# Rounded products that stream their columns from last to first

## What is computed

```python
for l in range(2):
    x = x + 0.5 * g1 * swiglu(modulate(x, sh1, sc1), ffn1_gate[l], ffn1_up[l], ffn1_down[l])
    x = x + g2 * token_mix(modulate(x, sh2, sc2), ...)       # w_in, gates, w_branch, w_out
    x = x + 0.5 * g3 * swiglu(modulate(x, sh3, sc3), ffn2_gate[l], ffn2_up[l], ffn2_down[l])
x = rms_norm(x) * final_norm
x = x + merged(rms_norm_2(x) @ w_in_2, ...) @ w_o_2          # four branches, gated and summed
x = x + square(relu(rms_norm_2(x) @ w_up_2)) @ w_down_2
```

## Time and profile before

| | |
|---|---|
| median of 3 runs | 3470.61 us (3468.1 to 3471.58) |
| span of the profiled execution | 3462.0 us, first to last instruction (the page gives no time of its own for it; the median lies 8.6 us above the span) |
| TensorE (PE) busy | 3417.4 us, 99% of the span |
| weight loads (PEld) busy | 2737.1 us, 79% |
| VectorE (DVE) / ScalarE (ACT) / GpSimd (POOL) busy | 51% / 35% / 8% |
| mean granted TensorE clock | 0.995 of full speed |
| DMA | 376.36 MB, a third of the 16 engines' span |

### The profile page before, as it was taken

How to read it: one execution, slowest core, us unless ns; L and a number is a source line. 1 busy time by engine, 2 the same in 40 slices (tenths; PEclk the granted TensorE clock), 3 DMA queues, 4 the chain that set the end, 5 groups by cost and what they waited for, 6 DMA issues and landing times.

```text
span 3462.0 us, 40836 instructions
## 1 busy us (share of the span) xinstructions
PE 3417.4 (99%) x16686; PEld 2737.1 (79%) x16686; DVE 1754.0 (51%) x3014; ACT 1197.3 (35%) x2021; POOL 263.1 (8%) x219
## 2 busy tenths in 40 slices
PE   8999999999999999999999999999999999999999
PEld 7888786778888788887767888888778777878887
DVE  7666446555565733334655643334453555364433
ACT  3222336543222332223555332224322444233322
POOL 0000210002000200011100100003011000120000
PEclk9999999999999999999999999999999999999999
DMA  7555322123565532323211322322222223122332
GB/s 253 203 208 192 108 84 69 41 71 112 190 228 194 183 100 95 104 86 117 74 44 31 105 90 83 106 87 96 77 79 68 76 67 122 39 96 90 98 103 79
DMA packets 120361, 376.36 MB, mean 109 GB/s; under 512 B 13296, under 2 KB 28272, under 8 KB 120176
## 3 DMA queue, kind: packets, MB, share of 16 engines
q1 hardware_dynamic: 120176, 373.76, 32.8%
HBM read 371.61 MB, written 2.10 MB: 108 GB/s over the span
## 4 chain that ended last, share of the span: by engine, by line
PE 93%; DVE 4%; ACT 2%; issue 0%; DMA 0%; POOL 0%; SPq 0%; DVEq 0%; ACTq 0%; POOLq 0%
PE ps L449 27%; PE ps L451 26%; PE ps L450 26%; PE ps L671 2%; PE ps L694 2%; PE ps L566 2%; PE ps L483 1%; PE ps L485 1%; PE ps L484 1%; PE ps L499 1%; DVE s_wl L1490 1%; PE ps L492 1%; ACT s_wh L969 0%; PE ps L536 0%; PE ps L537 0%
## 5 line engine op out<-in xcount | busy, mean ns | idle before, releaser
L1490 DVE TENSOR_TENSOR s_wl<-s_raw,s_wh 128x1024 fp32r<-128x1024 f32 (+3 forms) x645 | 705.7, 1095 | 885.2 <-ACT s_wh L969 878.7
L449 PE MATMUL ps<-s_uh,s_wh 128*128 128x512 f32 x2824 | 1128.5, 400 | 9.7 <-DVE s_ul L1551 3.8
L451 PE MATMUL ps<-s_ul,s_wh 128*128 128x512 f32 x2824 | 1104.2, 391 | 0.8 <-issue 0.8
L450 PE MATMUL ps<-s_uh,s_wl 128*128 128x512 f32 x2824 | 1103.4, 391 | 0.0
L969 ACT ACTIVATE s_wh<-s_raw 128x1024 fp32r<-128x1024 f32 (+3 forms) x645 | 588.1, 913 | 723.0 <-PE ps L451 535.4
L449 PEld LDWEIGHTS ps<-s_uh,s_wh 128*128 128x128 f32 x2824 | 532.2, 188 | 152.8 <-issue 40.2
L451 PEld LDWEIGHTS ps<-s_ul,s_wh 128*128 128x128 f32 x2824 | 531.7, 188 | 113.6 <-issue 1.2
L450 PEld LDWEIGHTS ps<-s_uh,s_wl 128*128 128x128 f32 x2824 | 532.5, 189 | 107.3 <-issue 2.7
L449 PE MATMUL ps<-s_fh,s_wh 128*128 128x512 f32 x960 | 378.6, 394 | 0.0
L451 PE MATMUL ps<-s_fl,s_wh 128*128 128x512 f32 x960 | 378.6, 394 | 0.0
L450 PE MATMUL ps<-s_fh,s_wl 128*128 128x512 f32 x960 | 378.6, 394 | 0.0
(11 more groups left out here) (419 smaller groups left out, 3337.9 us busy)
## 6 DMA issues: line engine op xcount, KB each, us to landing
s_raw<-w SPq DMA_DIRECT2D x616, 512.0 KB, 3.6
s_raw<-w SPq DMA_DIRECT2D x96, 192.0 KB, 2.4
s_raw<-w SPq DMA_DIRECT2D x64, 256.0 KB, 2.6
s_raw<-w SPq DMA_DIRECT2D x19, 128.0 KB, 2.0
s_x<-x SPq DMA_DIRECT2D x4, 512.0 KB, 6.7
out<-s_x SPq DMA_DIRECT2D x8, 256.0 KB, 2.2
s_raw<-w SPq DMA_DIRECT2D x4, 420.0 KB, 4.2
s_crow<-crow SPq DMA_DIRECT2D x2, 512.0 KB, 6.0
```

Of the source, the lines that this page charges most:

```text
L449: TE.matmul(o, w_hi(i, k), h, start=first, stop=False)
L450: TE.matmul(o, w_lo(i, k), h, start=False, stop=False)
L451: return TE.matmul(o, w_hi(i, k), l, start=False, stop=last)
L1490: V.tensor_tensor(wl[w][:, 0:n], raw[t % NRAW][:, 0:n], wh[w][:, 0:n].bitcast(F32), SUB).then_inc(*s_lo.up(("lo", t)))
```

## The change

A helper turns a view round in its last dimension, and every rounded product takes its moving operand and its output through it. The stationary operand stays as it was. So column 511 is streamed first and its results go to column 511 of the bank, then 510, and so on to 0 (279 to 0 for the short ones). Each column still meets the same weights and lands at the same place. The float32 products are left alone, and so are all readers of the banks.

```diff
+def back(t):
+    return t[:, ::-1]
...
         def three(o, i, k, h, l, first, last):
+            o, h, l = back(o), back(h), back(l)
             TE.matmul(o, w_hi(i, k), h, start=first, stop=False)
             TE.matmul(o, w_lo(i, k), h, start=False, stop=False)
             return TE.matmul(o, w_hi(i, k), l, start=False, stop=last)
...
-                        TE.matmul(o, h[:, k, sl(b)], w_hi(i, j), start=k == 0, stop=False)
-                        TE.matmul(o, l[:, k, sl(b)], w_hi(i, j), start=False, stop=False)
-                        ins = TE.matmul(o, h[:, k, sl(b)], w_lo(i, j), start=False, stop=k == nk - 1)
+                        TE.matmul(back(o), h[:, k, sl(b)], back(w_hi(i, j)), start=k == 0, stop=False)
+                        TE.matmul(back(o), l[:, k, sl(b)], back(w_hi(i, j)), start=False, stop=False)
+                        ins = TE.matmul(back(o), h[:, k, sl(b)], back(w_lo(i, j)), start=False, stop=k == nk - 1)
...
-                        TE.matmul(os[n][:], h, uh[:, k, :], start=k == 0, stop=False)
-                        TE.matmul(os[n][:], lo, uh[:, k, :], start=False, stop=False)
-                        ins = TE.matmul(os[n][:], h, ul[:, k, :], start=False, stop=k == 7)
+                        TE.matmul(back(os[n]), h, back(uh[:, k, :]), start=k == 0, stop=False)
+                        TE.matmul(back(os[n]), lo, back(uh[:, k, :]), start=False, stop=False)
+                        ins = TE.matmul(back(os[n]), h, back(ul[:, k, :]), start=False, stop=k == 7)
```

## The result

The changed kernel takes **3520.98 us** (median of 4, 3516.09 to 3523.46) against 3471.1 us before (median of 4, 3468.1 to 3481.73). The ratio is 1.0125, with a 95% interval of 1.0102 to 1.0149: slower by a little over one per cent. The profiled execution has a span of 3519.1 us, 57.1 us more than before. The forecast was no difference.

The account below looks back on a forecast made before the run. TensorE was taken to bound the kernel, through the start-to-start distance of 13,032 rounded products. Span 3462.0 + 0 for the change, plus 8.6 us from span to median, gave 3470.6 us; range 3,385 to 3,545 us.

Parts of the forecast that it names:

- The bound: Whole kernel: TensorE sets the time, PE busy 99% of the span, with 13,032 rounded products counted by start-to-start distance.
- Between these I take **zero: Rounded products: a descending stream adds nothing to the start-to-start distance, chosen between a 3,266 us floor and 5,060 us added.
- the fast kind: The 9,192 products of 512 columns whose distance lay 13.4 ns over 213.3 ns; the slow kind lay 20.0 ns over.
- the part that stays over: Rival, 512-column products: time beyond one tick a column grows, 9,192 x 6.6 ns = 61 us, giving 3,531 us; 15%.
- a start 2,044 bytes further on: In the 15% rival: a stream beginning at the tile's high end may have the dearer start everywhere, 6.6 ns more.
- It shrinks: Rival, rounded products: time beyond one tick a column falls, 24 us to 3,446 us or 86 us to 3,385 us; 19%.
- What spoke against it: Against the 15% rival: first-block distances are even from step to step, though s_uh and s_ul slices start at eight places.
- A lost pace: Rival, moving read or bank write: descending columns cost two ticks each, 2,784 us more, 6,255 us; 18%.
- The stepped load: L589 weight load, 31 columns 16 elements apart: 0.77 ns a column more; charged to 512-column products, 5,060 us, the far end.

Follow-up runs that it names:

- e15_b4: Changed kernel with s_uh and s_ul 4 bytes further on, so their first column read lies level with a weight slice's start modulo 256 bytes; 3554.91 us, timed once.
- e8_desc: Changed kernel with blocks of 16 columns streamed last to first, each block forward, read and write alike, tm() forward; 3532.65 us, ratio 1.0165.
- e3_pad_f: Kernel before, all streams forward, with 64 unused bytes per partition ahead of s_acc, moving s_fh and all later tiles; 3444.92 us, ratio 0.9913.
- e2_write: Changed kernel with, in the five feed-forward blocks, the moving operand read forward and only the bank written backward; 3473.63 us, ratio 0.9998 to the kernel before.
- e9_asc: Changed kernel with blocks of 16 columns in forward order, each backward inside, read and write alike, tm() forward; 3925.19 us, ratio 1.128.

## Why the prediction was wrong

**The bound** was right. PE sets the time, and 56.4 of the 57.1 us are in the distances between rounded products; no other engine moved.

**The step that failed** is "Between these I take **zero**". The reason given was that a backward stream reads the same neighbouring elements, each once. It looks at the moving operand alone, and so puts a term at nothing that the runs put at up to 6.6 ns a product. They show that the distance depends on how two operands lie to each other, and that of all the streams tried only a forward one level with the stationary operand has the cheap distance (226.7 ns). The change took that case away. The 9,192 products that the prediction counted as the fast kind rose, all but the 48 of `s_ch` in `tm`, which were dear already: by 4.2 to 6.6 ns in place of 0, 56.4 us in all.

**The rival that came true** is the part that stays over, at 3,531 us with 15%. Its sum, 9,192 x 6.6 = 61 us, against 57.1 of span and 49.9 between the medians, was right in size because its price was read from the earlier trace rows; it also gave the range its upper end, and only so does the measured 3520.98 us lie inside the range. Its mechanism was half right: the dearer kind everywhere, yes, but not through a start 2,044 bytes further on; e15_b4 begins level and is dear, and e8_desc is dear with each block forward; and the products of 280 columns, which by this rival should have risen by the same few ns, did not (130.7 and 130.3 ns). *It shrinks* (19%) did not come: no backward stream was cheaper than a forward one. The 24 us that it priced are there, but by placement (e3_pad_f, 3444.92 us), not by direction.

**What spoke against it was misread.** The prediction took the evenness of the earlier trace rows over eight slices as a sign that the place doesn't matter. The slices are 2,048 bytes apart, eight times 256, so they stand at one place in eight and could show nothing. The rows that did vary the place, against the earlier trace rows, were there, and the prediction had no account of what sets the two apart when it took zero.

**The clock, and what stays over.** From the earlier trace rows the prediction read one tick a column and a rest that stays over. At the upper level of the clock that stands, and no group's mean came nearer to the 213.3 ns of 512 bare columns than 226.7. But from the earlier trace rows it took the clock to be at that level throughout, and tenths over slices of 87 us can't show that. In a stretch of the trace before the granted clock is 0.50, the lower level of 1.2 GHz. The same 280-column products there, 11 steps from the first PE row to the last, and the stretch (columns as in the earlier trace rows):

```profile
478.46 0.44 PE L483 MATMUL ps<-s_wh,s_uh 128*128 128x280 f32 x1
478.47 0.33 PEld L484 LDWEIGHTS ps<-s_wh,s_ul 128*128 128x128 f32 x1
...
481.03 0.44 PE L485 MATMUL ps<-s_wl,s_uh 128*128 128x280 f32 x1
```

```profile
478.50:481.00 2.50, 2.50 (x12) 2.50 (x12) 0.00 (x0) 0.00 (x0) 1.79 (x2) 0.50 0.32 79
```

2.57 us, 233.6 ns each, and 280 columns at a tick of 1.2 GHz are 233.3: nothing stays over. (It is by chance the number of the dear 512-column product at the upper level.) The changed kernel has products of 512 columns, backward, in such a stretch, 11 steps:

```profile
2697.31 0.63 PE L455 MATMUL ps<-s_uh,s_wl 128*128 128x512 f32 x1
...
2702.00 0.63 PE L454 MATMUL ps<-s_uh,s_wh 128*128 128x512 f32 x1
```

```profile
2697.50:2701.90 4.40, 4.40 (x12) 3.43 (x11) 3.30 (x13) 0.00 (x0) 4.40 (x4) 0.50 0.02 4
```

4.69 us, 426.4 ns, and 512 columns at 1.2 GHz are 426.7. In the kernel before, forward and level, the median in such stretches is 427 ns too. So the rest, and with it the price of direction, shows at the upper level alone. It is no fixed number of TensorE's ticks, for 20.0 ns are 48 ticks at 2.4 GHz and would be 40 ns at 1.2. A limit that keeps its own time and hides behind the slower stream would look like this; that is argued, not shown.

**A lost pace** (18%) did not come. Writing backward costs nothing that shows (e2_write, ratio 0.9998). The rule of the Trainium skill that the prediction weighed (Advanced Engine Details and Errata, Memory Cachelines) says that any non-contiguous access pattern in PSUM slows matmuls significantly; the run shows no such slowing for a descending write, so a descending pair counts as contiguous if the rule holds here. Whether that rule is behind the 266.7 ns of e9_asc wasn't tried. The stepped load of the earlier trace rows had no bearing.

**What stays open** is what the two reads contend for. That the next weight load and the running stream meet, and keep out of each other's way only when they go through the same 256 bytes in step, fits the cheap place and the loss of it by direction. It was argued, not shown: no run took the weight load away, or turned it round, and it doesn't say why 64 bytes ahead costs 229.2 ns, why 4 bytes off costs more than 32, or why 16 bytes ahead and 16 behind differ.

## What to carry to other kernels

Where matmuls stand back to back, read the distance from start to start for each pair of operands; two values for one shape are a finding, and here 64 unused bytes that brought a tile level with the weights modulo 256 were worth 24 us by the distances, 0.7% (0.9% between the medians). Look at the granted clock of the very stretch before two distances are compared. Before an operand is said to stay the same "at eight places", compute the places modulo the period in question. And a stream's order belongs to the reading side: here turning the output cost nothing, and turning the input took away the one cheap case.

## What the runs showed of the chip

- At a granted clock of 1.00, a rounded product of 512 columns, stationary and moving operand level modulo 256 bytes and both read forward: 226.7 ns from start to start. Off by 32 to 224 bytes: 229.2 to 234.3 ns. The moving one 4 bytes ahead: 236.7 ns; 16 ahead 231.7, 16 behind 236.1.
- Moving operand read backward, at eight places 32 bytes apart: means of 233.3 to 236.6 ns; begun exactly level 235.6. Bank written backward: no difference.
- Blocks of 16 columns forward with each block backward inside, read and write alike: 266.7 ns; blocks backward with each forward inside: 233.4 ns with `s_uh`, 235.6 with `s_fh`, 237.7 with `s_qh`.
- At a granted clock of 0.50: 427 ns for 512 columns, forward or backward, and 233 for 280, which is one column per tick of 1.2 GHz with nothing over. The 280-column product is at 128.9 ns in a stretch at the upper level of the same trace.
